# The odd layer's output projection from seven half-size products for both pairs of blocks

## What is computed

```python
            z = hn @ od_w_in[j]
            q, k, v, g = _split(z, OD_SPLIT)
...
            mix = yc @ od_w_out[j]
        h = h + mix
        h = h + hier_moe(rms_norm(h, ffn_norm_g[i]), moe_w_group[i], moe_w_expert[i], moe_w_gate[i], moe_w_up[i], moe_w_down[i])
```

## Time and profile before

| | us |
|---|---|
| median of 3 runs | 1343.76 |
| lowest and highest run | 1342.78 and 1344.82 |
| profiled execution, its whole time | 1345.24 |
| its span from first to last instruction | 1343.3 |

### The profile page before, as it was taken

The page is one execution under the profiler, slowest core; times in us unless marked ns, Lnnn a source line. Parts: engine busy times, 40 slices in busy tenths (PEclk is TensorE's granted clock), DMA queues, the critical chain, the costliest instruction groups (busy, mean ns, idle before and its releaser), DMA issues.

```text
span 1343.3 us, 26339 instructions
## 1 busy us (share of the span) xinstructions
PE 1058.4 (79%) x10962; PEld 628.8 (47%) x10962; DVE 412.1 (31%) x884; ACT 179.7 (13%) x429; POOL 90.7 (7%) x227
## 2 busy tenths in 40 slices
PE   6999988666677667679999999988666765776578
PEld 5885444333344334344688554445333433433343
DVE  1694323112112111226674544432111111121116
ACT  2344311000000000011121000221000000000001
POOL 0100011000000000000110100011000000000000
PEclk9999999888888888899999999999888888888889
DMA  9846799999999999999454236699999999999992
GB/s 360 322 162 245 293 406 427 428 428 428 428 428 428 429 429 429 428 414 367 153 188 148 103 126 239 279 395 426 428 428 429 429 428 428 428 427 429 429 421 100
DMA packets 57841, 474.88 MB, mean 354 GB/s; under 512 B 4057, under 2 KB 6105, under 8 KB 32193
## 3 DMA queue, kind: packets, MB, share of 16 engines
q1 hardware_dynamic: 56800, 470.32, 84.9%
q10 hardware_dynamic: 768, 2.57, 0.5%
q0 software_dynamic: 224, 1.31, 0.3%
HBM read 473.12 MB, written 3.16 MB: 355 GB/s over the span
## 4 chain that ended last, share of the span: by engine, by line
DMA 49%; PE 45%; DVE 2%; issue 2%; ACT 1%; SPq 1%; POOL 0%; DVEq 0%; ACTq 0%; POOLq 0%
DMA big<-in_moe_w_up_dram 48%; PE ps L920 10%; PE ps L663 7%; PE ps L1105 5%; PE ps L686 4%; PE ps L1019 3%; PE ps L654 3%; PE ps L733 2%; PE ps L644 2%; PE ps L1167 2%; PE ps L942 1%; PE ps L831 1%; PE ps L950 1%; SPq L527 1%; PE ps L848 1%
## 5 line engine op out<-in xcount | busy, mean ns | idle before, releaser
L920 PE MATMUL ps<-big 128*32 128x256 f32 x4064 | 322.6, 485 | 161.2 <-DMA big<-in_moe_w_up_dram 161.0
L920 PEld LDWEIGHTS ps<-big 128*32 128x32 f32 x4064 | 166.1, 138 | 312.5 <-issue 179.7
L1741 DVE SCALAR_TENSOR_TENSOR big<-big,ps 64x256 f32<-64x256 f32 x64 | 26.4, 413 | 684.0 <-ACT big L1361 684.0
L942 PE MATMUL ps<-big 128*32 128x256 f32 x2048 | 123.8, 382 | 57.5 <-DVE big L1750 57.5
L942 PEld LDWEIGHTS ps<-big 128*32 128x32 f32 x2048 | 59.9, 109 | 107.6 <-DVE big L1750 74.4
L950 PE MATMUL ps<-big 32*128 32x256 f32 x1024 | 73.3, 398 | 41.9 <-ACT big L1372 40.6
L1361 ACT ACTIVATE big<-ps 64x256 f32<-64x256 f32 x64 | 24.2, 378 | 568.6 <-PE ps L920 568.6
L663 PE MATMUL ps<-big,xT 128*128 128x512 f32 x224 | 98.2, 593 | 1.3 <-ACT xT L1214 1.3
L950 PEld LDWEIGHTS ps<-big 32*128 32x128 f32 x1024 | 49.5, 184 | 70.8 <-issue 70.8
L2164 POOL TENSOR_TENSOR big<-big,rk 128x64 f32<-128x64 f32 x64 | 19.0, 296 | 775.0 <-PE ps L929 745.4
L890 PE MATMUL ps<-xn,big 128*32 128x256 f32 x1056 | 69.3, 379 | 0.0
(11 more groups left out here) (251 smaller groups left out, 1011.3 us busy)
## 6 DMA issues: line engine op xcount, KB each, us to landing
big<-in_moe_w_gate_dram SPq DMA_DIRECT2D x64, 2048.0 KB, 33.1
big<-in_moe_w_down_dram SPq DMA_DIRECT2D x62, 2048.0 KB, 38.7
big<-in_moe_w_up_dram SPq DMA_DIRECT2D x60, 2048.0 KB, 37.3
big<-in_od_w_in_dram SPq DMA_DIRECT2D x12, 2048.0 KB, 13.0
big<-in_ev_w_in_dram SPq DMA_DIRECT2D x6, 2048.0 KB, 20.7
big<-in_ple_w_gate_dram SPq DMA_DIRECT2D x8, 1024.0 KB, 19.1
big<-in_od_w_out_dram SPq DMA_DIRECT2D x4, 2048.0 KB, 7.8
big<-in_moe_w_up_dram SPq DMA_DIRECT2D x6, 1024.0 KB, 35.4
```

The source lines that it names most:

```text
L920: ins = nc.tensor.matmul(ps[TOK * i:TOK * i + TOK, 5, 0:2 * P].rearrange("p (b n) -> p b n", b=2), xe[:, k, :], (low if k < KD // 2 else w ...
L942: ins = nc.tensor.matmul(ps[TOK * q:TOK * q + TOK, 7, 0:QD], hidT[:, k, :], wd[:, k, q * QD:(q + 1) * QD], start=k == 0, stop=k == KF - 1)
```

## The change

Both pairs of blocks are now made from seven products. TensorE adds the products of the second pair onto those of the first in the same seven banks, so the sums on ScalarE and VectorE afterwards are made once, as before. `out_block(0)` and `out_block(1)` are gone, and with them the bank `rout_11`.

- In step 10 TensorE runs products a and a2 of the first pair (`out_begun`). Behind the loop it runs `gain_rows(1)`, then b, d, c, b2, c2 of the first pair, then a, b, d, c, a2, b2, c2 of the second.
- VectorE makes the first tile of the first pair in step 8, its other two tiles and four sums in step 10 (`out_parts(0)`), and behind the loop `gain_diagonals(1)`, the last tile of the first pair, and all of the second pair's but its last tile, which stands where it stood.
- The tiles and sums of the second pair are written over those of the first, so VectorE waits for the products that read them (`out_read`).
- SyncE waits for five counts of `out_read` for slots 0 and 1.
- The banks of the last jobs change: `last_a` is bank 2, `rout_01` bank 4, `rout_10` bank 5. The first transposition of `moe(1)` (`ffnT1_00`) takes bank 4 in both kernels; it was `rout_10`'s before.

```diff
-LAST_BANKS = {"last_b": "yT3_0", "last_d": "yT3_1", "last_c": "gain1"}
+LAST_BANKS = {"rout_01": "yT3_0", "rout_10": "yT3_1"}
+OUT_READS = "b", "d", "c", "b2", "c2"
...
-    rout = [f"rout_{t}{n}" for t in range(2) for n in range(2)]
     for i in range(HEAD_STEPS):
-        jobs += rout if i == HEAD_STEPS - 2 else []
+        jobs += ["last_a", "rout_00"] if i == HEAD_STEPS - 2 else []
...
-    jobs += ["gain1"] + [f"last_{i}" for i in "abdc"]
+    jobs += ["gain1"] + [f"last_{i}" for i in "bdc"] + ["rout_01", "rout_10"]
...
-        BLOCK_READ = {"out0": 1, "rout0": 2, "rout1": 3}
+        BLOCK_READ = {"out0": 1}
...
+                elif name in ("rout0", "rout1"):
+                    sync.wait_ge(out_read, len(OUT_READS))
...
-                            sync.wait_ge(out_tiles_ready, 4)
+                            sync.wait_ge(out_tiles_ready, 8)
...
+            out_banks = {}
+
+            def out_product(pair, i, job):
+
+                B11, T1, B21, B22 = out_quarters(pair)
+                A11, A21, A12, A22 = out_rows[pair]
+                lhs, rhs = {"a": (A11, B11), "a2": (A12, B21), "b": (OS1, T1), "d": (OS2, OT2), "c": (OS3, OT3),
+                            "b2": (OS4, B22), "c2": (A22, T1)}[i]
+                sums, tiles = {"a": (0, 0), "a2": (0, 0), "b": (1, 1), "d": (2, 2), "c": (3, 3), "b2": (4, 0), "c2": (4, 4)}[i]
+                if sums:
+                    pe.wait_ge(out_sums_ready, 4 * pair + sums)
+                if tiles:
+                    pe.wait_ge(out_tiles_ready, 4 * pair + tiles)
+                if pair == 0:
+                    out_banks[job] = begin(job)
+                for k in range(HALF):
+                    ins = nc.tensor.matmul(out_banks[job], lhs[:, k, :], rhs[:, k, :], start=k == 0 and pair == 0,
+                                           stop=k == HALF - 1 and pair == 1, skip_group_check=True)
+                if pair == 1:
+                    end(job, ins)
+                elif i in OUT_READS:
+                    ins.then_inc(out_read, 1)
+
+            def out_begun():
+
+                for c in range(2):
+                    arrived(f"rout{c}")
+                    for t in range(NT):
+                        taken(pe, f"yT{c}_{t}")
+                out_product(0, "a", "last_a")
+                out_product(0, "a2", "rout_00")
...
-                    out_block(0)
+                    out_begun()
...
-            out_block(1)
             gain_rows(1)
+            for i, job in (("b", "last_b"), ("d", "last_d"), ("c", "last_c"), ("b2", "rout_01"), ("c2", "rout_10")):
+                out_product(0, i, job)
             for c in (2, 3):
                 for t in range(NT):
                     taken(pe, f"yT{c}_{t}")
                 arrived(f"rout{c}")
-            B11, OT1, B21, B22 = out_quarters()
-            OT4 = OT1
-
-            def out_product(job, lhs, rhs, fresh=True):
-
-                b = begin(job) if fresh else bank(job)
-                for k in range(HALF):
-                    ins = nc.tensor.matmul(b, lhs[:, k, :], rhs[:, k, :], start=k == 0 and fresh, stop=k == HALF - 1,
-                                           skip_group_check=True)
-                end(job, ins)
-
-            out_product("last_a", OA11, B11)
-            pe.wait_ge(block_read, BLOCK_READ["rout1"])
-            pe.sem_inc(bank_full[BANK["rout_11"]], 1)
-            pe.wait_ge(out_sums_ready, 4)
-            pe.wait_ge(out_tiles_ready, 3)
-            out_product("last_b", OS1, OT1)
-            out_product("last_d", OS2, OT2)
-            out_product("last_c", OS3, OT3)
-            out_product("rout_00", OA12, B21, False)
-            out_product("rout_01", OS4, B22, False)
-            pe.wait_ge(out_tiles_ready, 4)
-            out_product("rout_10", OA22, OT4, False)
+            for i, job in (("a", "last_a"), ("b", "last_b"), ("d", "last_d"), ("c", "last_c"), ("a2", "rout_00"),
+                           ("b2", "rout_01"), ("c2", "rout_10")):
+                out_product(1, i, job)
...
+            def out_tile(pair, out, left, right, after):
+
+                if after:
+                    dve.wait_ge(out_tiles_ready, 4 * pair + after)
+                ve.tensor_tensor(out, left, right, ALU.subtract).then_inc(out_tiles_ready, 1)
+
+            def out_first_tile(pair):
+
+                for c in (2 * pair, 2 * pair + 1):
+                    dve.wait_ge(landed[loads.at[f"rout{c}"]], 16 * loads.turn[f"rout{c}"])
+                B11, B12, B21, B22 = out_quarters(pair)
+                out_tile(pair, B12, B12, B11, 0)
+
+            def out_sum(pair, out, left, right, op, after):
+
+                if after:
+                    dve.wait_ge(out_sums_ready, 4 * pair + after)
+                ve.tensor_tensor(out, left, right, op).then_inc(out_sums_ready, 1)
+
+            def out_given(pair, i):
+
+                if pair:
+                    dve.wait_ge(out_read, OUT_READS.index(i) + 1)
+
+            def out_parts(pair):
+
+                B11, T1, B21, B22 = out_quarters(pair)
+                A11, A21, A12, A22 = out_rows[pair]
+                out_given(pair, "b")
+                out_sum(pair, OS1, A21, A22, ALU.add, 0)
+                out_given(pair, "d")
+                out_sum(pair, OS2, OS1, A11, ALU.subtract, 1)
+                out_tile(pair, OT2, B22, T1, 1)
+                out_given(pair, "c")
+                out_sum(pair, OS3, A11, A21, ALU.subtract, 0)
+                out_tile(pair, OT3, OT2, B11, 2)
+                out_given(pair, "b2")
+                out_sum(pair, OS4, A12, OS2, ALU.subtract, 2)
...
+                if hd == NH:
+                    out_first_tile(0)
                 if hd == NH + GATE_LAG:
-                    for c in (2, 3):
-                        dve.wait_ge(landed[loads.at[f"rout{c}"]], 16 * loads.turn[f"rout{c}"])
-                    ve.tensor_tensor(OT3, B22, B12, ALU.subtract).then_inc(out_tiles_ready, 1)
-                    ve.tensor_tensor(B12, B12, B11, ALU.subtract).then_inc(out_tiles_ready, 1)
-                    dve.wait_ge(out_tiles_ready, 2)
-                    ve.tensor_tensor(OT2, B22, B12, ALU.subtract).then_inc(out_tiles_ready, 1)
+                    out_parts(0)
                 n = hd - BACK_LAG
                 if 0 <= n < NH:
                     odd_back(n // 2, n % 2)
+            gain_diagonals(1)
+            dve.wait_ge(out_read, 1)
+            B11, T1, B21, B22 = out_quarters(0)
+            out_tile(0, T1, B21, OT2, 3)
...
+            out_first_tile(1)
             for c in (2, 3):
                 for t in range(NT):
                     taken(dve, f"yT{c}_{t}")
-            ve.tensor_tensor(OS1, OA21, OA22, ALU.add).then_inc(out_sums_ready, 1)
-            ve.tensor_tensor(OS3, OA11, OA21, ALU.subtract).then_inc(out_sums_ready, 1)
-            dve.wait_ge(out_sums_ready, 2)
-            ve.tensor_tensor(OS2, OS1, OA11, ALU.subtract).then_inc(out_sums_ready, 1)
-            dve.wait_ge(out_sums_ready, 3)
-            ve.tensor_tensor(OS4, OA12, OS2, ALU.subtract).then_inc(out_sums_ready, 1)
-            gain_diagonals(1)
+            out_parts(1)
+            B11, T1, B21, B22 = out_quarters(1)
...
-            ve.tensor_tensor(B12, B21, OT2, ALU.subtract).then_inc(out_tiles_ready, 1)
+            out_tile(1, T1, B21, OT2, 3)
...
-            full(dve, "rout_11")
-            dve.wait_ge(block_read, BLOCK_READ["rout1"])
             ve.tensor_tensor(h22, h22, OP5, ALU.add).then_inc(out_parts_used, 1)
-            dve.wait_ge(out_parts_used, 1)
-            emptied("rout_11", ve.tensor_tensor(h22, h22, bank("rout_11"), ALU.add))
```

16 lines of the change are left out of this document (5 added, 11 removed).

## The result

| | before | after |
|---|---|---|
| median of 12 runs each, taken side by side | 1343.60 us | 1346.66 us |
| lowest and highest run | 1342.76 and 1346.40 | 1343.32 and 1348.54 |
| ratio after to before, 95% interval | | 1.0018, 1.0010 to 1.0026 |
| profiled execution and its span | 1345.24 and 1343.3 | 1346.60 and 1344.7 |

The change makes the kernel slower by 2.4 us (1.3 to 3.5) by the ratio; the two medians stand 3.06 us apart. A second comparison of the same two kernels, made later beside the experiments (12 runs against 23), gave 1.0023 (1.0015 to 1.0032), 3.1 us. The forecast was 2.9 us and 1346.7 us.

A forecast was written before the change was run, and what follows sets the result against it. TensorE's chain up to the projection's end was taken to bound the kernel. Wait less saved matmuls +0.9, clock +2.2 and bank -0.2 gave +2.9 us on 1343.76, so 1346.7 us, range 1344.0 to 1348.5 us.

The forecast's parts named there:

- What bounds the kernel: TensorE sets the pace before 865 us, then weights fill the DMA; moving the projection's end moves the kernel's end in full.
- the first wait for weights near 922: Sign of being right: the same shift there as at the last product's end, 2.5 to 3.5 us later than 862.80.
- Matmuls saved: Plain blocks' 32 matmuls become 28 for the first pair; four fewer on TensorE's path, 3.44 us less work.
- The wait: TensorE idle ahead of `gain_rows` until VectorE finishes `gain_diagonals`: 4.36 us; less the matmuls saved, +0.9 us carried.
- The clock: TensorE's clock falls to half behind the new wait at `gain_rows`: 2.2 us, ends 1.4 and 2.9.
- the clock stays full: Rival: no clock fall behind the wait at `gain_rows`, leaving +0.9 - 0.2 = +0.7, 1344.5 us; chance 0.15.
- The bank: Experts' first transposition takes `rout_01`'s long-free bank and can start up to 0.6 us earlier; 0.2 us taken, ends 0 and 0.6.
- What hides the rest: VectorE's extra tiles and sums, some 11.2 us, and SyncE's later transfers into slots 0 and 1 cost nothing.
- the rival of a second loss: Another second-pair product waits for a tile or bank, or the clock falls again: another 2 us or so, 1348.7 us; chance 0.10.
- that of a small wait: VectorE reaches `gain_diagonals` earlier; faster if the wait falls below 3.4 us, with none 1340.1 us; chance 0.05.
- The sum: Whole kernel: +0.9 + 2.2 - 0.2 us, 2.9 us slower, median 1346.7 us, at the border of the 2.7 us detectable.

The follow-up runs named there:

- the run with the filler: Changed kernel with five throwaway matmuls on TensorE ahead of its wait for the gains; ratio to the kernel before 1.0004 (0.9996 to 1.0013), +0.5 us.
- the longer wait: Changed kernel with VectorE writing the gains three times instead of once; ratio to the kernel before 1.0049 (1.0033 to 1.0064), +6.6 us.
- the run with the gains written first: Changed kernel with VectorE's gains write moved to the head of step 10; ratio to the kernel before 0.9980 (0.9970 to 0.9989), median 1339.94 us.
- the gains between the tiles: Changed kernel with the gains written behind the first pair's third tile, ahead of the last sum and both copies out; ratios to before 0.9985 and 1.0001.
- The same kernel compared twice: Changed kernel with the gains written behind the first pair's third tile, compared with the kernel before in two sets of runs; ratios 0.9985 and 1.0001.

## Why the prediction was right

**What bounds the kernel.** Right. TensorE's chain sets the start of the stream of weights, and the delay passes in full: +10.29 us gave +10.2. In the twelve profiled executions the time from the end of the last product to the end of the span is 479.7 us in the mean, 478.7 to 480.5, while that end itself moved over 13.4 us. The slope of the span on it is 0.93. The two profiled executions of before and after stand at its two ends, 480.5 and 478.7, so their spans differ by 1.4 us instead of 3. An end that moves by less than the projection's was one of the forecast's signs of being wrong; over all twelve executions it is not borne out. In the kernel after the same weights that released the wait at 950.84 came at 951.61, 0.8 us later, though SyncE's issues had moved by 2.9. The traces show where an execution wins or loses such an us: from the end of the last product to the first wait for weights it is 88.04 us in the kernel before (950.84 less 862.80) and 85.61 in the kernel after (951.61 less 866.00), the longest and the shortest of the twelve (mean 86.9), and from there to the end of the span 392.5 and 393.1 (392.4 to 393.7 in all). The kernel after, profiled again, has 87.43 for the first part, so the 85.61 is not the change's; what makes it vary stays open. The forecast looked for its shift "at the first wait for weights near 922": there is none near 922 in either trace, and at the first there is the shift is hidden in this scatter.

**Matmuls saved.** Right: 3.44 forecast, 3.44 measured once nothing stood in the way.

**The wait.** Right in place, in who releases it and in size: 4.36 forecast, 4.16 measured. The start of `gain_rows` was placed 12.10 us behind the head of step 10 and came 12.06 behind it, so the seven intervals on VectorE were well chosen. The 0.2 us lie at the other end: I took the transpositions from start to start, 0.87, where TensorE counts as idle only from their end.

**The clock.** Right that the clock falls and that this costs one to three us: 2.2 forecast from the mean of four rows, 2.25 and 2.29 measured, and 2.19 by the run with the filler. That the size came out to a tenth is luck. The four rows themselves ran from 1.39 to 2.92, and with small changes to the wait the same term measured 1.43 to 2.43. The working left open what sets the size, and thought of the length of the wait only as a condition. The runs show it: 1.43 behind 6.67 us of idle time, 1.70 behind 2.36, 2.43 behind 3.90. The price is about half of the time that TensorE works at half clock: it resumed at 821.70 and the clock came back at 826.4, half of 4.7 is 2.35; with the longer wait 823.41 and 826.4, 1.5.

**The rival "the clock stays full"** was given 0.15 since 2.23 us of idle time had not lowered it. That row was rightly held to be weak evidence, for a wait twice as long. TensorE at two waits for weights in the kernel after, and a stretch of 1 us in the middle of the first:

```profile
951.61 5.35 PE L922 MATMUL ps<-big 128*32 128x256 f32 x64 [2.25 <-DMA big<-in_moe_w_up_dram]
...
995.66 3.66 PE L922 MATMUL ps<-big 128*32 128x256 f32 x64 [2.21 <-DMA big<-in_moe_w_up_dram]
```

```profile
954.00:955.00 1.00, 1.00 (x16) 0.57 (x12) 0.00 (x0) 0.00 (x0) 0.00 (x0) 0.50 0.96 410
```

Behind 2.25 us of idle time the 64 records take 5.35 us in place of 3.66, behind 2.21 us they take 3.66; and at 1289.30 in the same trace they take 5.35 behind 2.21 too. The twelve traces hold 575 waits for weights of over 2 us ahead of such a full group. All 24 of 2.05 to 2.19 us left the clock at full, of the 36 of 2.20 to 2.29 us 15 left it and 21 lowered it, and all 515 of 2.30 to 5.19 us lowered it. So the rows of the kernel before could have spoken more plainly: of its 48 such waits 43 lowered the clock, and the five that did not were of 2.14 to 2.23 us. At 4.36 us the rival had nothing for it, and 0.15 was too much.

**The bank.** Right in direction, 0.2 forecast, 0.29 measured. The first transposition came 0.49 earlier behind the last product (0.45 in place of 0.94). The routing product behind it came 0.38 earlier, 3.18 behind the last product instead of 3.56: here ScalarE's scaling held it, as argued. The row, kernel after:

```profile
867.97 1.12 ACT L1336 ACTIVATE xT<-ps,kept 128x128 f32<-128x128 f32 x4
```

It ends at 869.09 and the routing product starts at 869.18.

**What hides the rest.** Right, by the run with the gains written first. In the kernel after TensorE has no idle time between the gains and the end of the last product, so the rival of a second loss did not come about; nor did that of a small wait, which asked for less than 3.4 us.

**The sum.** +2.9 forecast; +3.04 - 0.29 = +2.75 by the trace, +2.4 and +3.1 by the ratios. By terms: wait less saving +0.9, measured 0.85 (the run with the filler); clock +2.2, measured 2.2; bank -0.2, measured -0.29. It lies at the border of 2.7 us, as the forecast said: the first ratio, 1.0018, is just within 0.2%, the second, 1.0023, just above.

## What to carry to other kernels

When a change shortens the chain of the engine that bounds a kernel, look at what the removed work was covering: here 13.8 us of matmuls had hidden a small VectorE instruction at the end of a long queue, and the wait for it cost more than the saving. The cure was not to make less work for VectorE but to move the one instruction that TensorE asks for first to the front, or the four small matmuls that need it behind work that is ready. And price a new wait of TensorE amid dense matmuls, from about 2.2 us on, with a surcharge for the clock: 1.4 to 2.4 us at this place, 1.2 to 3.0 among the experts. It is a range and not a number, and a longer wait does not make it larger in step.

## What the runs showed of the hardware

- The granted clock fell to 0.50 behind waits of 2.25, 2.35 and 2.36 us and stayed at 1.00 behind others of 2.21 and 2.23. Of 575 waits for weights in the twelve traces none up to 2.19 us lowered it and each from 2.30 us on did; between the two it went either way, so there the length of the wait alone does not decide it. The Trainium skill, page "TensorE: Matmul & The Clock Gate", section "Why this matters for your kernels", advises against idle gaps between bursts of matmuls; these rows agree, and they show the fall at shorter waits than those that the page names.
- The clock can fall behind the wait: with the gains between the tiles TensorE had resumed at 816.27, and the fall is in the stretch 817 to 818 (0.71). The cost does not grow in step with the wait: of the waits for the gains it was least, 1.43 us, behind the longest, 6.67 us, and among the experts of the kernel before 3.38 us of idle time cost 2.92 us and 5.00 us cost 1.91.
- Ten records of throwaway matmuls (4.46 us) in place of the idle time kept the clock at full, and were worth 2.19 us of the projection.
- The same kernel compared twice gave 0.9985 and 1.0001, with intervals of 0.0010 and 0.0008 either way that overlap by 0.0003 only. A difference of 0.1% between two kernels of different sets of runs says nothing here.
